# Combining two experts' rows: both choices stacked in the partitions, one matmul per half tile, and scaling two tiles behind

## The chip, the cores and the metric

The kernel runs on one core of a Trainium2 chip. The metric is the device time of one launch in microseconds. Three runs of the kernel before took 2286.6, 2289.5 and 2290.79 us; the median is 2289.5 us. The profile is of one further execution, which took 2287.02 us and whose span in the profile is 2285.2 us.

## The reference, cut to what matters

The model is one layer of a decoder: a mixing part (window attention and a gated delta rule), then a mixture of experts, then a final norm. The change touches only the last step, in which each token's two expert outputs are weighed, summed, added to the residual `h` and normed:

```python
y_buf = lax.map(expert_block, ...)                      # h @ w_down for blocks of 128 rows
y = jnp.zeros((N, D), jnp.float32).at[tok_buf].add(     # two rows for each token
    y_buf.reshape(P, D).astype(jnp.float32) * gate_buf[:, None])
hp = hp + y
y_prompt = rmsnorm(hp, norm_final)                      # x * rsqrt(mean(x*x) + EPS) * gain
```

There are 2048 prompt tokens and 64 sample tokens of width 1024, in float32: 16 tiles of 128 tokens and one of 64, 17 in all.

## The kernel before, in words

The kernel has three stages: a projection, the mixing part, and `moe` (from line 2656). `moe` sorts tokens by expert, runs 66 blocks of 128 rows through the experts (a gate and up product at L3208, a down product at L3217), and writes each result row with an indirect DMA (L2911) to its place in a DRAM tensor `S["y"]`. That tensor holds every token's first choice in one range of rows and every token's second choice in another.

When the last of these writes has landed, ACT signals `experts_stored` (L3004), and the combine begins. This is the stage that the change touches. For each tile `t` of 17:

- SP issues `fetch(t)` (L2832): one DMA brings the rows of 128 tokens, both choices, from `S["y"]` into `pair[t % 8]`, token in the partition, choice as the outer index of the free dimension. It is 1024 KB, in rows of 4 KB, and half of that for the last tile of 64 tokens. Eight buffers stand ready, so eight fetches are issued at once. `fetch(t + 8)` waits until tile `t` has been read (`weighted`).
- ACT makes two diagonal matrices of the 128 tokens' weights, one for each choice (L3011).
- PE (`weigh`, L3243) multiplies: for each half of the 1024 columns, the first choice's rows by the first diagonal and then, accumulating, the second choice's rows by the second. A float32 product shows as two LDWEIGHTS and two MATMUL records, called passes here, so a full tile is 8 passes and the kernel 136. There are four pairs of PSUM banks, so tile `t` waits for `summed` of tile `t - 4`.
- DVE (`add`, L3163) adds `h` and writes `out[t % 8]`. From tile 8 on it waits until the store that used this buffer 8 tiles ago has landed (`stored`).
- ACT squares and sums the row (L3025), POOL makes the root (L2960, L2962).
- DVE scales by the root and the gain (`scale`, L3169). It does this `BEHIND = 4` tiles after the add: after `add(t)` comes `scale(t - 4)`, and after the last add come four more scales.
- SP stores the tile (L2842). SP's program is one list: `fetch(t + 8)`, then `store(t - 4)`, then the same for the next `t`. All fetches and stores go through SP's one queue.

Of the kernel before, what the change touches and what calls it, by code (L numbers as in the profile page):

```python
# [12 lines left out]
ALU = mybir.AluOpType  # L13
ACT = mybir.ActivationFunctionType
AX = mybir.AxisListType.X

P = 128
D = 1024
# [8 lines left out]
HD = 64  # L27
# [2628 lines left out]
def moe(nc, A, S, O, K):  # L2656
# [8 lines left out]
    with Phase(nc, "p5_") as ctx:  # L2665
# [34 lines left out]
        midt = [cut(y_arena, (4 + b) * DE, (FC, P)) for b in two]  # L2700

        CB, OB = 8, 8
        BEHIND = 4
        kept = range(BEHIND + 1)
        pair = [cut(w_arena, 2 * c * D, (2, D)) for c in range(CB)]
        ya = [[pair[c][:, k, :] for c in range(CB)] for k in range(2)]
        out = [cut(w_arena, (2 * CB + c) * D, (D,)) for c in range(OB)]

        n3 = LAST[1] - LAST[0]
# [30 lines left out]
        spare = sb("spare", [P, 3])  # L2740
        home = [sb(f"home{b}", [P, 1], I32) for b in two]
        gain = cut(y_arena, 0, (D,))
        diag = [[cut(y_arena, D + (2 * b + k) * P, (P,)) for k in range(2)] for b in two]
        half = sb("half", [P, 2 * H])
        ss, ms, rs = ([sb(f"{n}{c}", [P, 1]) for c in kept] for n in ("ss", "ms", "rs"))
        ps = ctx.psum([P, 8, 512])
# [26 lines left out]
        def _(sp):  # L2773
# [27 lines left out]
                load_weights(j, j, j % R)  # L2801
            sp.wait_ge(K["ids_out"], 16 * 2 * TILES)
            sp.wait_ge(on["owner_ready"], 1)
            h_flat = h_all[:].rearrange("p t d -> p (t d)")
            with sp.Fori(3 * R, NE - R, R) as i:
                for b in ring:
# [21 lines left out]
            def fetch(t):  # L2828
                r, c = n_rows(t), t % CB
                if t >= CB:  # L2830
                    sp.wait_ge(on["weighted"], t - CB + 1)
                sp.dma_start(pair[c][0:r], S["y"][0:2 * HOMES].rearrange("(k t p) d -> t p k d", k=2, p=P)[t][0:r]  # L2832
                             ).then_inc(gathered[c], 16)

            for t in two:
                fetch(t)
# [131 lines left out]
        @block.scalar  # L2968
        def _(act):
            act.wait_ge(on["shifted"], 1)  # L2970
            nc.scalar.activation(last.ex, last.ex, ACT.Exp).then_inc(on["exps"], 1)

            def gate(j, b):
                act.wait_ge(gu_done.sem, gu_done.all(j))
                act.wait_ge(mid_ready.sem, mid_ready.back(j, 2))
                nc.scalar.activation(th[b], ps[:, 2 + b, 0:DE], ACT.Tanh, scale=0.5).then_inc(th_ready.sem, 1)  # L2976

            def evacuate_y(j, b, sent):
                act.wait_ge(down_done.sem, down_done.all(j))
                act.wait_ge(y_out[b], sent)  # L2980
                nc.scalar.copy(y[b][:, 512:], ps[:, 1 if b else 6, :]).then_inc(y_act.sem, 1)  # L2981

            def blocks(i, first=0):
                for n in range(first, R):
                    gate(i + n, n % 2)
                    evacuate_y(i + n - 1, (n + 1) % 2, 8 * i + 16 * ((n + 1) // 2))

            gate(0, 0)
            act.wait_ge(on["owner_ready"], 1)
            with nc.allow_non_contiguous_dma(reason="the owners of the blocks to one row"):  # L2990
                act.dma_start(owner[0:1, 0:2 * SPILL].rearrange("o (p c) -> o p c", c=2), owner_c[0:SPILL]).then_inc(on["owner_in"], 16)
            act.dma_start(owner[0:1, 2 * SPILL:], total_c[0:1, :]).then_inc(on["owner_in"], 16)
            act.sem_inc(on["owner_in"], 16)
            blocks(0, 1)
            with act.Fori(R, NE - R, R) as i:
                blocks(i)
            total = n_blocks(act)
            with act.Fori(NE - R, total, R) as i:
                blocks(i)
            evacuate_y(total - 1, 1, total * 8)  # L3000
            for b in two:
                act.wait_ge(y_out[b], total * 8 + 16)
            apart(act, on["owner_in"], 48)
            act.sem_inc(on["experts_stored"], 1)  # L3004

            def weights(t):
                n = t if t < SAMPLES else SAMPLES if t == NT else t + 1
                if t >= 2:
                    act.wait_ge(on["weighted"], t - 1)
                for k in range(2):  # L3010
                    nc.scalar.activation(diag[t % 2][k], ident[:], ACT.Copy, scale=w[:, n, k:k + 1]).then_inc(on["diag_ready"], 1)  # L3011

            for t in two:
                weights(t)
            for t in range(T):
                c = t % len(kept)
                if t + 2 < T:
                    weights(t + 2)
                act.wait_ge(on["summed"], t + 1)
                if t >= len(kept):  # L3020
                    act.wait_ge(on["rs_ready"], t - len(kept) + 1)
                if t:
                    act.wait_ge(on["squared"], t)
                r = n_rows(t)
                nc.scalar.activation(y[0][0:r], out[t % OB][0:r], ACT.Square, accum_out=ss[c][0:r]).then_inc(on["squared"], 1)  # L3025

        @block.vector
        def _(dve):
# [124 lines left out]
            with dve.Fori(NE - R, total, R) as i:  # L3153
                blocks(i)
            evacuate_y(total - 1, 1, total * 8)
            dve.wait_ge(on["h_in"], 16 * (NE // R - 2))

            def add(t):
# [22 lines left out]
        @block.tensor  # L3181
        def _(pe):
            mm, tr = nc.tensor.matmul, nc.tensor.transpose
            pe.wait_ge(on["both_ready"], 1)
            pe.wait_ge(on["zero_ready"], 1)
            pe.wait_ge(on["sums_in"], 32)
            earlier(mm, ps[:, 3, :], last, upto, ones).then_inc(on["counted"], 1)

            pe.wait_ge(on["lists_in"], 16)
            mm(ps[:, 7, 0:NE], lists, ident[0:NE, 0:NE], start=True, stop=False)  # L3190
            pe.wait_ge(on["at_ready"], 1)
            for n in range(n3):
                for k in range(2):
                    t = mm(ps[:, 7, 0:NE], at_lane[:, n, k, :], at_block[:, n, k, :], start=False, stop=(n == n3 - 1 and k == 1))  # L3194
            t.then_inc(on["listed"], 1)
            pe.wait_ge(on["sel_ready"], 1)
            pe.wait_ge(on["token_ready"], 1)
            for g in range(4):
                t = mm(ps[:, 4, g * NE:(g + 1) * NE], sel[:, g].rearrange("p q b -> p (q b)"), token, start=True, stop=True)  # L3199
            t.then_inc(on["spread"], 1)  # L3200

            def gate_up(j, b, bw, arrived):
                pe.wait_ge(xt_ready.sem, xt_ready.all(j))
                pe.wait_ge(mid_ready.sem, mid_ready.back(j, 2))
                pe.wait_ge(gate_in[bw], arrived)
                pe.wait_ge(up_in[bw], arrived)
                for c in range(KC):
                    t = mm(ps[:, 2 + b, :], xt[b][:, c, :], w_gu[bw][:, :, c, :], start=(c == 0), stop=(c == KC - 1))  # L3208
                t.then_inc(gu_done.sem, 1)

            def down(j, b, bw, arrived):
                pe.wait_ge(midt_ready.sem, midt_ready.all(j))
                pe.wait_ge(down_in[bw], arrived)
                for n in two:
                    pe.wait_ge(y_act.sem if n else y_vec.sem, y_vec.back(j, 2))
                    for c in range(FC):
                        t = mm(ps[:, n if b else 5 + n, :], midt[b][:, c, :], w_dn[bw][:, c, n * 512:(n + 1) * 512],  # L3217
                               start=(c == 0), stop=(c == FC - 1))
                    t.then_inc(down_done.sem, 1)

            def blocks(i, first=0):
                for n in range(first, R):
                    gate_up(i + n, n % 2, n, 4 * i + 16)
                    down(i + n - 1, (n + 1) % 2, (n - 1) % R, 4 * i + (16 if n else 0))

            gate_up(0, 0, 0, 16)
            blocks(0, 1)
            with pe.Fori(R, NE - R, R) as i:
                blocks(i)
            total = n_blocks(pe)  # L3230
            with pe.Fori(NE - R, total, R) as i:
                blocks(i)
            down(total - 1, 1, R - 1, total * 4)

            def weigh(t):
                c, r, at = t % CB, n_rows(t), 2 * (t % 4)
                pe.wait_ge(on["diag_ready"], 2 * t + 2)
                pe.wait_ge(gathered[c], 16 * (t // CB + 1))
                if t >= 4:
                    pe.wait_ge(on["summed"], t - 3)  # L3240
                for n in two:
                    for k in range(2):
                        ins = mm(ps[0:r, at + n, :], diag[t % 2][k][0:r, 0:r], ya[k][c][0:r, n * 512:(n + 1) * 512],  # L3243
                                 start=(k == 0), stop=(k == 1))
                ins.then_inc(on["weighted"], 1)

            for t in range(T):
                weigh(t)
# [78 lines left out]
```

## Time and profile before

| what | us |
|---|---|
| median of three runs | 2289.5 |
| the profiled execution's own time | 2287.02 |
| its span | 2285.2 |
| busy in the span: PE, DVE, ACT, POOL | 2168.0, 1296.6, 548.6, 612.7 |
| the combine: first fetch issued | 2203.56 |
| the combine: first matmul, last matmul ends | 2208.49, 2270.08 |
| the last scaling ends | 2277.3 |

How to read it: times are from the span's start. The busy time of PE is that of matmuls. The DMA share is the mean busy share of the core's 16 DMA engines in a stretch, and GB/s what they moved. The granted clock of TensorE is given as a part of its full 2.4 GHz.

### The profile page before, as it was taken

To read this page: it belongs to the slowest core of one execution; us is meant where nothing else is said; L and a number is where in the kernel's file an instruction comes from. 1 tells how busy PE (TensorE), PEld (TensorE's weight loads), DVE (VectorE), ACT (ScalarE), POOL (GpSimd) and SP (SyncE) were. 2 spreads that over 40 slices of the span, in tenths; PEclk is the share of its full clock that TensorE was granted. 3 is DMA by queue.
4 is the path that set the end of the run, shared out by engine and by line. 5 is a ranking of instruction groups with operands and counts; after the bars stand their busy time and mean duration, and the time that the engine had idled before them with its cause. 6 is when DMAs were issued, how large, how long until landed. Compare 5 with 4: busy or idle time off the path is not lost. (4 is left out here: it accounts for less than half of the span.)

```text
span 2285.2 us, 47478 instructions
## 1 busy us (share of the span) xinstructions
PE 2168.0 (95%) x18764; PEld 1176.5 (51%) x18764; DVE 1296.6 (57%) x2674; ACT 548.6 (24%) x1421; POOL 612.7 (27%) x804
## 2 busy tenths in 40 slices
PE   7999999999988899999999999839999999999977
PEld 4444544544545666666766666524444444444433
DVE  4524425313524666556676867357767676776736
ACT  3302202202213344334434444200000001010013
POOL 1100200100200100300131221246555555555452
PEclk9999999999998899999999999959999999999988
DMA  9051040230075532233223221159999999999957
GB/s 323 20 148 38 24 148 28 51 115 13 5 206 154 134 101 70 64 86 102 75 65 117 74 65 55 58 228 357 351 373 363 370 365 379 367 383 369 346 206 307
DMA packets 171954, 405.90 MB, mean 178 GB/s; under 512 B 51188, under 2 KB 92772, under 8 KB 147162
## 3 DMA queue, kind: packets, MB, share of 16 engines
q1 hardware_dynamic: 141847, 349.34, 43.5%
q0 software_dynamic: 23648, 35.19, 4.2%
q10 hardware_dynamic: 6274, 18.72, 2.1%
q8 instruction: 139, 2.28, 0.4%
q14 instruction: 46, 0.37, 0.0%
HBM read 344.98 MB, written 94.80 MB: 192 GB/s over the span
## 5 line engine op out<-in xcount | busy, mean ns | idle before, releaser
L3208 PE MATMUL p_ps<-p_w_arena,k_room 128*128 128x512 f32 x1024 | 451.7, 594 | 10.8 <-DVE k_room L3110 10.8
L3208 PEld LDWEIGHTS p_ps<-p_w_arena,k_room 128*128 128x128 f32 x1024 | 195.3, 191 | 256.5 <-issue 245.5
L2864 POOL DMA_INDIRECT k_room<-s_hn,p_slot x272 | 276.4, 1016 | 123.7 <-issue 72.0
L2474 PE MATMUL p_ps<-k_room,p_mixt 128*128 128x512 f32 x544 | 263.5, 614 | 0.0
L3132 DVE STREAM_TRANSPOSE p_y_arena<-p_y_arena 32x64 f32<-32x64 f32 x1024 | 241.0, 235 | 13.2
L902 PE MATMUL p_ps<-k_room,p_w 128*128 128x512 f32 x544 | 240.6, 598 | 0.0
L902 PE MATMUL p_ps<-p_xt,p_w 128*128 128x512 f32 x544 | 238.1, 593 | 0.5 <-DVE p_xt L721 0.5
L3217 PE MATMUL p_ps<-p_w_arena,p_y_arena 128*128 128x512 f32 x512 | 231.9, 596 | 3.5 <-DVE p_y_arena L3132 3.5
L902 PEld LDWEIGHTS p_ps<-k_room,p_w 128*128 128x128 f32 x544 | 102.0, 191 | 124.1 <-issue 122.1
L902 PEld LDWEIGHTS p_ps<-p_xt,p_w 128*128 128x128 f32 x544 | 101.5, 190 | 122.6 <-issue 120.3
L3217 PEld LDWEIGHTS p_ps<-p_w_arena,p_y_arena 128*128 128x128 f32 x512 | 97.8, 191 | 127.3 <-issue 127.3
L3110 DVE STREAM_TRANSPOSE k_room<-k_room 128x1024 f32<-128x1024 f32 x66 | 134.0, 2030 | 13.3 <-DMA k_room<-s_hn,p_slot 11.4
L2474 PEld LDWEIGHTS p_ps<-k_room,p_mixt 128*128 128x128 f32 x544 | 94.6, 190 | 83.7 <-issue 79.1
L731 DVE TENSOR_SCALAR p_y<-p_ext,p_w_conv 128x512 f32<-128x512 f32 x48 | 23.4, 486 | 195.0 <-ACT p_ext L579 195.0
L2976 ACT ACTIVATE p_y_arena<-p_ps 128x256 f32<-128x256 f32 x64 | 24.6, 384 | 440.9 <-PE p_ps L3208 380.7
L2911 POOL DMA_INDIRECT s_y<-k_room,p_home x66 | 68.6, 1039 | 196.1 <-DMA s_y<-k_room,p_home 80.2
L579 ACT COPY p_ext<-p_ps 128x512 f32<-128x512 f32 x48 | 28.1, 586 | 358.0 <-PE p_ps L902 357.9
L3116 DVE SCALAR_TENSOR_TENSOR p_y_arena<-p_y_arena,p_ps 128x256 f32<-128x256 f32 x64 | 26.9, 420 | 148.6 <-ACT p_y_arena L2976 144.9
L735 DVE SCALAR_TENSOR_TENSOR p_y<-p_ext,p_w_conv,p_y 128x512 f32<-128x512 f32 x144 | 108.3, 752 | 5.1
L1517 POOL TENSOR_SCALAR p_ms<-p_ss 128x8 f32<-128x8 f32 x17 | 3.4, 199 | 338.4 <-DVE p_ss L1969 338.4
L522 POOL TENSOR_SCALAR p_ms<-p_ss 128x1 f32<-128x1 f32 (+1 forms) x17 | 6.9, 407 | 296.7 <-ACT p_x L562 196.1
L2981 ACT COPY k_room<-p_ps 128x512 f32<-128x512 f32 x64 | 37.5, 586 | 199.6 <-PE p_ps L3217 187.4
(442 smaller groups left out, 3002.2 us busy)
## 6 DMA issues: line engine op xcount, KB each, us to landing
p_w_arena<-in_w_exp_gate SPq DMA_DIRECT2D x64, 1024.0 KB
p_w_arena<-in_w_exp_up SPq DMA_DIRECT2D x64, 1024.0 KB
p_w_arena<-in_w_exp_down SPq DMA_DIRECT2D x64, 1024.0 KB
p_w_arena<-s_y SPq DMA_DIRECT2D x16, 1024.0 KB, 14.7
p_x<-in_x_prompt SPq DMA_DIRECT2D x30, 512.0 KB, 4.8
s_kv<-p_us SPq DMA_DIRECT2D x32, 256.0 KB
s_kq<-p_y SPq DMA_DIRECT2D x32, 256.0 KB, 3.0
p_kq<-s_kq SPq DMA_DIRECT2D x16, 512.0 KB, 5.8
```

The costliest lines, as they stand in the source:

```text
L579: nc.scalar.copy(ext[q % 3][:, CW - 1:], ps[:, job % 4, :]).then_inc(freed_act.sem, 1)
L735: ins = stt(y[:, c, :], src[:, k:k + SN], w_conv[:, c, k:k + 1], y[:, c, :], ALU.mult, ALU.add)
L902: ins = mm(ps[:, job % 4, :], columns(at, at + P)[:, c], xt[s % 2][:, c, :], start=(c == 0), stop=(c == KC - 1))
L2474: ins = mm(ps[:, 7 - n, :], mixt[t % 2][:, c, :], w_out[:, c, n * 512:(n + 1) * 512], start=(c == 0), stop=(c == KC - 1))
L2864: pool.indirect_dma_start(out=x[b][:, 256 * g:256 * g + 256], out_offset=None, in_=S["hn"].rearrange("t (q k) -> (t q) k", q=4), in_offset ...
L2911: pool.indirect_dma_start(out=S["y"], out_offset=bass.IndirectOffsetOnAxis(ap=home[b][:, 0:1], axis=0), in_=y[b], in_offset=None, bounds_c ...
L2981: nc.scalar.copy(y[b][:, 512:], ps[:, 1 if b else 6, :]).then_inc(y_act.sem, 1)
L3110: nc.vector.transpose(xt[b].rearrange("p c (g r) -> p g c r", g=4), x[bx].rearrange("p (g a c) -> p g c a", g=4, c=KC)).then_inc(xt_ready. ...
L3116: nc.vector.scalar_tensor_tensor(mid[b], th[b], 1.0, ps[:, 2 + b, 0:DE], ALU.add, ALU.mult).then_inc(mid_own.sem, 1)
L3132: t = nc.vector.transpose(midt[b][32 * q:32 * q + 32, :, 32 * g:32 * g + 32], mid[b][32 * g:32 * g + 32].rearrange("p (q a c) -> p q c a", ...
L3208: t = mm(ps[:, 2 + b, :], xt[b][:, c, :], w_gu[bw][:, :, c, :], start=(c == 0), stop=(c == KC - 1))
L3217: t = mm(ps[:, n if b else 5 + n, :], midt[b][:, c, :], w_dn[bw][:, c, n * 512:(n + 1) * 512], start=(c == 0), stop=(c == FC - 1))
```

## The change

A tile is cut into two groups of 64 tokens. `fetch(t)` becomes two DMAs, one for each choice: choice 0 of all the tile's tokens goes to partitions 0 to 63 and choice 1 to partitions 64 to 127, with the group of 64 as the outer index of the free dimension. `weigh` then needs one product for each group and half of the columns, with a stationary operand of 128 rows and 64 columns that holds both choices' weights. Its result goes to 64 partitions of PSUM, the first group's to the lower half and the second group's to the upper. For this ACT makes, in place of two diagonals of 128 columns, two operands of 64 columns from `lanes` (two 64 by 64 identities, one above the other). The weights have to stand in the other half of the partitions too: SP moves them across with two small DMAs (`w_turned`), and DVE puts them together in `w_pair` with four small copies behind `experts_stored`. `BEHIND` goes from 4 to 2.

```diff
-        BEHIND = 4
+        BEHIND = 2
         kept = range(BEHIND + 1)
         pair = [cut(w_arena, 2 * c * D, (2, D)) for c in range(CB)]
-        ya = [[pair[c][:, k, :] for c in range(CB)] for k in range(2)]
...
-        diag = [[cut(y_arena, D + (2 * b + k) * P, (P,)) for k in range(2)] for b in two]
+        diag = [cut(y_arena, D + 2 * HD * b, (2, HD)) for b in two]
+        lanes = cut(y_arena, D + 4 * HD, (HD,))
+        w_pair = cut(y_arena, D + 5 * HD, (T, 2))
+        w_other = cut(K["base"][:], 0, (T, 2))
...
             sp.wait_ge(on["owner_ready"], 1)
+            for a in two:
+                sp.dma_start(w_other[a * HD:(a + 1) * HD].rearrange("p t k -> p (t k)"),
+                             w[(1 - a) * HD:(2 - a) * HD].rearrange("p t k -> p (t k)")).then_inc(on["w_turned"], 16)
...
-                sp.dma_start(pair[c][0:r], S["y"][0:2 * HOMES].rearrange("(k t p) d -> t p k d", k=2, p=P)[t][0:r]
-                             ).then_inc(gathered[c], 16)
+                halves = r // HD
+                for k in two:
+                    sp.dma_start(pair[c][k * HD:(k + 1) * HD, 0:halves],
+                                 S["y"][0:2 * HOMES].rearrange("(k t a p) d -> k t p a d", k=2, a=2, p=HD)[k, t, :, 0:halves]
+                                 ).then_inc(gathered[c], 16)
...
-                for k in range(2):
-                    nc.scalar.activation(diag[t % 2][k], ident[:], ACT.Copy, scale=w[:, n, k:k + 1]).then_inc(on["diag_ready"], 1)
-
+                for a in two:
+                    nc.scalar.activation(diag[t % 2][:, a], lanes, ACT.Copy, scale=w_pair[:, n, a:a + 1]).then_inc(on["diag_ready"], 1)
+
+            act.wait_ge(on["lanes_ready"], 1)
+            act.wait_ge(on["w_paired"], 4)
...
+            dve.wait_ge(on["experts_stored"], 1)
+            tt(lanes, ident[:, 0:HD], ident[:, HD:], ALU.add).then_inc(on["lanes_ready"], 1)
+            dve.wait_ge(on["w_turned"], 32)
+            for k in two:
+                here = slice(k * HD, (k + 1) * HD)
+                nc.vector.tensor_copy(w_pair[here, :, k], w[here, :, k]).then_inc(on["w_paired"], 1)
+                nc.vector.tensor_copy(w_pair[here, :, 1 - k], w_other[here, :, k]).then_inc(on["w_paired"], 1)
             dve.wait_ge(on["h_in"], 16 * (NE // R - 2))
...
-                pe.wait_ge(gathered[c], 16 * (t // CB + 1))
+                pe.wait_ge(gathered[c], 32 * (t // CB + 1))
...
                 for n in two:
-                    for k in range(2):
-                        ins = mm(ps[0:r, at + n, :], diag[t % 2][k][0:r, 0:r], ya[k][c][0:r, n * 512:(n + 1) * 512],
-                                 start=(k == 0), stop=(k == 1))
+                    for a in range(r // HD):
+                        ins = mm(ps[a * HD:(a + 1) * HD, at + n, :], diag[t % 2][:, a], pair[c][:, a, n * 512:(n + 1) * 512],
+                                 start=True, stop=True)
```

## Rows read from the trace of the kernel before

**Rows 1.** The chain that ended last: start us, us, what

```profile
2203.56 4.79 DMA p_w_arena<-s_y
...
2208.49 61.59 PE p_ps L3243 x136
...
2270.10 1.22 DVE p_w_arena L3163
2271.32 4.78 DVE p_w_arena L3169 x4
2276.10 1.20 DVEq L2665
```

**Rows 2.** Stretches: length; busy PE, PEld, DVE, ACT, POOL; PEclk, DMA share, GB/s

```profile
2208.50:2250.00 41.50, 41.50 (x90) 18.25 (x91) 19.40 (x16) 19.09 (x42) 15.73 (x39) 0.93 1.03 404
2260.00:2270.00 10.00, 10.00 (x24) 3.54 (x22) 7.83 (x7) 5.39 (x12) 2.97 (x8) 1.00 0.47 191
```

**Rows 3.** DMA issues of the combine: queue, count, KB each, us to landing

```profile
p_w_arena<-s_y SPq DMA_DIRECT2D x16, 1024.0 KB, 14.7
out_y_prompt<-p_w_arena SPq DMA_DIRECT2D x16, 512.0 KB, 3.4
p_y_arena<-in_norm_final SPq DMA_DIRECT2D x1, 512.0 KB, 8.3
p_w_arena<-s_y SPq DMA_DIRECT2D x1, 512.0 KB, 14.4
```

**Rows 4.** SP's issues in time: a store and the last fetch

```profile
2241.51 0.35 SPq L2842 DMA_DIRECT2D out_y_prompt<-p_w_arena  x1
2242.49 0.65 SPq L2832 DMA_DIRECT2D p_w_arena<-s_y  x1
```

**Rows 5.** PE by line, shapes kept apart: busy us, mean ns of one

```profile
L3243 PE MATMUL p_ps<-p_w_arena,p_y_arena 128*128 128x512 f32 x128 | 58.0, 617 | 10.6 <-DMA p_w_arena<-s_y 10.6
...
L2455 PE MATMUL p_ps<-p_pt,p_av 128*64 128x512 f32 x128 | 31.1, 606 | 0.0
...
L960 PE MATMUL p_ps<-p_w,p_xt 128*64 128x512 f32 x64 | 14.2, 595 | 0.0
```

**Rows 6.** Stretches of 1 us around the last fetch's arrival

```profile
2253.00:2254.00 1.00, 1.00 (x4) 0.50 (x3) 0.06 (x1) 0.64 (x3) 0.74 (x2) 1.00 1.09 352
2254.00:2255.00 1.00, 1.00 (x4) 0.45 (x3) 0.00 (x0) 0.00 (x0) 0.00 (x0) 1.00 1.10 242
2255.00:2256.00 1.00, 1.00 (x3) 0.38 (x2) 0.47 (x1) 0.00 (x0) 0.00 (x0) 1.00 0.91 258
2256.00:2257.00 1.00, 1.00 (x4) 0.49 (x3) 1.00 (x2) 0.21 (x1) 0.00 (x0) 1.00 1.01 414
```

**Rows 7.** Stretches of 1 us while the mixing part loads `w_out` in half tiles

```profile
723.00:724.00 1.00, 1.00 (x12) 1.00 (x14) 0.00 (x0) 0.26 (x1) 0.00 (x0) 0.50 1.05 213
724.00:725.00 1.00, 1.00 (x8) 0.84 (x8) 0.83 (x2) 0.00 (x0) 0.00 (x0) 0.50 1.03 205
725.00:726.00 1.00, 1.00 (x8) 0.84 (x6) 1.00 (x3) 0.00 (x0) 0.00 (x0) 0.51 0.98 197
...
728.00:729.00 1.00, 0.58 (x6) 0.17 (x2) 1.00 (x3) 0.00 (x0) 0.00 (x0) 1.00 0.97 240
```

**Rows 8.** The scaling's group on DVE by line: busy us, mean ns

```profile
L3169 DVE SCALAR_TENSOR_TENSOR p_w_arena<-p_w_arena,p_rs,p_y_arena 128x1024 f32<-128x1024 f32 (+1 forms) x17 | 21.4, 1275 | 0.0
```

**Rows 9.** In order of time: an add, its tile's root; the last tile's root

```profile
2228.76 1.23 DVE L3163 TENSOR_TENSOR p_w_arena<-p_ps,p_h_all 128x1024 f32<-128x1024 f32 x1 [2.21 <-PE p_ps L3243]
...
2231.53 0.55 POOL L2962 TENSOR_TENSOR p_rs<-p_ms,p_half 128x1 f32<-128x1 f32 x1
...
2273.91 1.47 POOL L2962 TENSOR_TENSOR p_rs<-p_ms,p_half 64x1 f32<-64x1 f32 x1
```

**Rows 10.** A small operation on DVE; ACT's diagonals of the first two tiles

```profile
1496.10 0.19 DVE L3041 TENSOR_REDUCE p_h_all<-p_h_all 128x4 f32<-128x32 f32 x1 [0.51 <-ACT p_h_all L2971]
...
2203.62 1.28 ACT L3011 ACTIVATE p_y_arena<-k_ident,k_w 128x128 f32<-128x128 f32 x4 [5.00 <-DMA s_y<-k_room,p_home]
```

## The prediction

> **What bounds the kernel now.** I read the chain of waits first, then the stretches of the combine, then the DMA issues. The chain [rows 1] shows the combine as one piece: the last scattered row lands, the first fetch takes 4.79 us, PE runs 61.59 us without a gap (x136 passes), and then DVE does one add and queued scalings until 2277.30 (2276.10 + 1.20). What follows, up to the end of the span, is 7.9 us of last store and closing (2285.2 - 2277.3), which the change leaves alone. So PE sets the pace. But the stretches [rows 2] show a second limit just under it: from 2208.5 to 2250 the DMA share is 1.03, at 404 GB/s. Only behind the fetches does it fall: 0.47 from 2260 to 2270. The combine's bytes [rows 3] are 16 fetches of 1.049 MB, one of 0.524, the gain's 0.524 and 16.5 stores of 0.524: 26.5 MB, or 65.6 us at 404 GB/s, against PE's 61.6. Two nearly equal limits lie on top of each other: whoever halves one finds the other. The last fetch is issued at 2242.49 [rows 4] and lands 14.4 us later [rows 3], at 2256.9, 13.2 us before PE is done with it.
>
> **The matmuls.** Before, 128 passes of 128 columns are 58.0 us, 0.453 each; the busy time of a group counts overlapping records once. The trace has passes of the new form, alternating between the two halves of the columns: 128 of 128*64 in 31.1 us and 64 in 14.2 us [rows 5], so 0.243 and 0.222 each, while one record's mean (606 and 595 ns) is hardly shorter than that of a full one (617). The two halves run side by side. The new combine has 16 x 8 + 4 = 132 passes: 29 to 32 us in place of 61.6. A tile goes from 8 x 0.453 = 3.6 us to 1.8 to 1.95. Alone, that takes 30 us from PE, and none of it can come off the end beyond what the DMA allows.
>
> **The fetches.** A fetch moves the same bytes in the same 4 KB rows, but as two DMAs of 64 partitions each. That form stands in the trace. The last fetch has 64 tokens and so 64 partitions, [64, 2, 1024] like each new half. Around its arrival [rows 6] the rate is 352, 242 and 258 and then back at 414, with the DMA share still at 0.91 to 1.10: engines busy, moving less. The bytes missing against 410 GB/s, between the mean of the combine and the row behind, are 58 + 168 + 152 = 378 KB, which is 0.92 us on top of 1.28: 0.524 MB took 2.20 us, 238 GB/s. The second place is `w_out`, of which four loads of 512 KB go to 64 partitions each, first twice the lower and then twice the upper half: 205, 197 and later 240 GB/s [rows 7], with the DMA share about 1. So a load to half of the partitions runs at 197 to 258 GB/s. I take 240: the last fetch lies, like each new one, between transfers that don't use only its half, while `w_out` has two of the same half in a row. Ends for the range: 205 GB/s (one of the two slow rows, where the other is a little lower still), and 404, if consecutive DMAs to opposite halves overlap fully.
>
> By the page "SBUF — State Buffer" of the Trainium skill (section "Door 1: The DMA port swizzle (why `[64,N]` ≈ `[32,N]`)"), partitions 0 to 63 reach only 8 of the 16 ports; the two slow places of this trace agree. Its section "Can I just issue two DMAs to hit both halves?" says no, with only 6% over a single one: 1.06 x its 196 GB/s is 208 GB/s, an estimate by that page that would put the sum where the first rival below stands. No row here has two opposite halves in alternation.
>
> **Where that leads.** The 16 full fetches (16.78 MB) take 41.5 us at 404 and 69.9 at 240: +28.4. The DMA queue never runs dry, as eight tiles are asked for ahead and PE now waits for each (at 240 GB/s a tile and its store take 4.4 + 1.3 = 5.7 us, PE 1.9, or twice that if the clock falls to 1.2 GHz in the gaps; DVE 1.22 + 1.27; all of it is covered). Since SP's list has `store(t - 2)` in place of `store(t - 4)`, six stores stand ahead of `fetch(16)` and not four: +2 x 1.3 = +2.6. The last fetch itself is two DMAs of 64 partitions, before one: unchanged. It lands at 2256.9 + 28.4 + 2.6 = 2287.9.
>
> Behind it: `add(14)` needs buffer 6 back, so `store(6)`, next in the queue, landed: 2289.2. DVE then does add(14), scale(12), add(15), scale(13), add(16), at 1.22 [rows 1] and 1.27 [rows 8] each: 6.2, until 2295.4. Two scalings follow (2.5) while ACT and POOL make the last root. Before, the root came 4.06 us after the add (ended 2271.32 [rows 1], root 2273.91 + 1.47 [rows 9]), with POOL slow beside DVE's four scalings; with two I take 3.4 (bounds 4.1 and 2.1, an undisturbed one: add ended 2229.99, root 2232.08 [rows 9]). The last scaling ends at 2295.4 + 3.4 + 1.3 = 2300.1, against 2277.3: **+22.8 us**.
>
> **The scaling two behind.** By itself it takes two of the four queued scalings (2.5 us) from the end and gives most back to the wait for the root: 5.97 us from add to end before, 4.7 after, a gain of 1.3; with the bounds 0.6 to 2.2, the lower by 4.1 + 1.27, the upper where the two scalings' 2.5 end last. It is in the sum.
>
> **Small edits.** SP issues two small DMAs at the start of the expert stage, ahead of block 12's weights, and 17 more fetch DMAs, at 0.35 to 0.65 us each [rows 4]; SP has waits of several us between them, the weights are four blocks ahead: 0 to 1 us, I take 0. DVE's five small operations after `experts_stored` (0.19 each [rows 10], about 0.3 with their semaphores, 1.5 in all) and ACT's first four operands (before 1.28 [rows 10]) come before the first matmul, some 3 us of work under the first fetch's 4.79 [rows 1]: 0. If the cover were gone it would cost 3. In the other direction they could gain nothing, since the fetch is longer than before. The second issue of the first fetch, 0.4, I take as within the 28.4.
>
> **The rivals.**
> 1. *The halves hold to the slowest rate.* At 205 GB/s the fetches take 81.9 us, +40.4 in place of +28.4: **+34.8 us**. For it: the rows of `w_out` and the page above. Against: the last fetch, and 240 in the third row of `w_out`.
> 2. *The engines drift apart.* If the 16 DMA engines need not move in step, one that is a few rows ahead is already on the other half, and it and the one behind no longer hinder each other. At 300 GB/s the fetches take 55.9: +14.4, in all **+8.8 us**. For it: the rows of `w_out` rise from 197 to 240 in three us [rows 7]. Against: after 50 us of traffic the last fetch still showed a sharp dip [rows 6].
> 3. *Opposite halves overlap fully (the other side).* Then the fetches take 41.5. The last lands at 2256.9 + 2.6 - 0.9 = 2258.6, the same 12.2 us follow (2300.1 - 2287.9), end 2270.8: **-6.5 us**. It decides from 16.78 MB / (41.5 + 5.6) = 356 GB/s up, where the sum is zero. For it: bytes and row sizes are the same. Against: the share of busy engines stays at 1 while the rate falls [rows 6, 7].
> 4. *It doesn't do what it says*: the columns' halves run one after another and the fetches at full rate. PE keeps its pace of 0.453 a pass, the last tile has 4 passes fewer (-1.8) and the end gains 1.3: **-3 to 0**, nearly the same. The overlap of the trace speaks against it [rows 5]; under slow fetches it would cost nothing.
>
> **How the numbers follow.** Chances: my forecast (220 to 270 GB/s, +17 to +29) 0.50; rival 1 0.18; rival 2 (270 to 350, +1 to +16) 0.18; rival 3 0.09; rival 4 0.05. The profiled execution took 2287.02, so 2309.8 by the sum; the runs' median lies 2.5 above it, and I give the time against the median: 2289.5 + 22.8 = 2312.3. Range 2294 (+4.5: leaves out rivals 3 and 4 and the edge of 2) to 2326 (rival 1 with 1.5 more). A difference under 0.2% (4.6 us) can't be told from none: faster 0.09, same 0.07 (most of rival 4 and the edge of rival 2), slower 0.84.
>
> **What would show it.** After the change: the rate in the combine at 240 to 300 GB/s (fetches and stores mixed) with the DMA share still at 1; PE busy 29 to 32 us in a stretch of 80 to 90, with waits for `s_y` fetches before nearly every tile and a clock at times at half; a tile every 5.7 us; the adds of tiles 8 to 13 ending right behind a fetch, `scale(16)` some 12 us after the last landing. Wrong if the combine's rate stays at 400, or if PE still runs without gaps.

## The result and the profile after

Over four runs of each, one after another on the same chip, the changed kernel took 2319.2 us (2311.31 to 2320.8) and the kernel before 2288.99 (2286.6 to 2290.79): ratio 1.0131, 95% interval 1.0113 to 1.0148, or **30.2 us slower**. The forecast was 2312.3, the range 2294 to 2326. The profiled execution took 2319.02 with a span of 2317.2, 32.0 over that of before.

I measure the combine from the issue of its first fetch to the end of its last scaling. Before: 2203.56 to 2277.30, 73.7 us [rows 1]. After: 2206.07 to 2308.54, 102.5 us. So 28.7 of the 32.0 lie in it. Another 2.5 lie ahead of it, 1.7 of them already there at the expert stage's first matmul (1532.78 against 1531.08), in code that the change leaves alone. The other 0.8 arose in the expert stage, where the change adds two small DMAs; one execution differs from another by several us up to this point, so no run here says whether they had a part in it, and I count none of the 2.5 as the change's. The remaining 0.8 lies behind the last scaling.

Stretches of the combine after (length; busy PE, PEld, DVE, ACT, POOL; then PEclk, DMA share and GB/s), for [rows 2]:

```profile
2210.00:2220.00 10.00, 4.90 (x12) 1.45 (x14) 1.23 (x1) 1.66 (x4) 7.22 (x18) 0.50 1.05 233
2220.00:2260.00 40.00, 20.90 (x64) 5.07 (x62) 15.72 (x13) 12.83 (x31) 7.97 (x18) 0.80 1.04 216
2260.00:2290.00 30.00, 17.07 (x46) 4.36 (x48) 10.89 (x10) 6.51 (x16) 2.97 (x8) 0.67 1.03 270
2290.00:2300.00 10.00, 6.74 (x16) 1.45 (x12) 6.13 (x6) 4.41 (x10) 1.50 (x5) 0.67 1.02 366
```

This is the whole result in four rows. The share of busy DMA engines is what it was (1.04 against 1.03), and the bytes per second have halved (216 against 404). The share says that the engines are occupied, not that they move much. From 2260 on stores are mixed in, which use all partitions, and the mean rises (270, then 366). PE went from fully busy to about half, and its granted clock from 0.93 to between 0.50 and 0.80.

The DMA issues of the combine after (queue, count, KB each, us to landing), for [rows 3]:

```profile
p_w_arena<-s_y SPq DMA_DIRECT2D x32, 512.0 KB, 24.4
out_y_prompt<-p_w_arena SPq DMA_DIRECT2D x16, 512.0 KB, 20.3
p_w_arena<-s_y SPq DMA_DIRECT2D x2, 256.0 KB, 20.9
```

Sixteen fetches of 1024 KB have become 32 of 512 KB, and a store now takes 20.3 us to land where it took 3.4: it stands behind up to eight tiles of slow fetches in the same queue. The groups of the new combine (line, engine, operation, count | busy us, mean ns | idle before, and what ended it), for [rows 5] and [rows 8]:

```profile
L3260 PE MATMUL p_ps<-p_w_arena,p_y_arena 128*64 128x512 f32 x132 | 50.6, 875 | 50.2 <-issue 27.7 <-DMA p_w_arena<-s_y 20.1 <-ACT p_y_arena L3019 2.4
L3186 DVE SCALAR_TENSOR_TENSOR p_w_arena<-p_w_arena,p_rs,p_y_arena 128x1024 f32<-128x1024 f32 (+1 forms) x17 | 21.7, 1276 | 1.4 <-POOL p_rs L2970 1.4
L3180 DVE TENSOR_TENSOR p_w_arena<-p_ps,p_h_all 128x1024 f32<-128x1024 f32 (+1 forms) x17 | 20.8, 1223 | 59.3 <-PE p_ps L3260 32.5 <-DMA out_y_prompt<-p_w_arena 26.8
```

PE has 132 passes, as counted, and is idle 50.2 us. DVE's operations last what they lasted (1276 and 1223 ns), but its adds wait 26.8 us for stores. Three tiles on PE, eight records each, at two clocks:

```profile
2213.88 3.68 PE L3260 MATMUL p_ps<-p_w_arena,p_y_arena 128*64 128x512 f32 x8 [13.67 <-DMA p_w_arena<-s_y]
2218.78 3.68 PE L3260 MATMUL p_ps<-p_w_arena,p_y_arena 128*64 128x512 f32 x8 [1.22 <-DMA p_w_arena<-s_y]
2230.98 1.94 PE L3260 MATMUL p_ps<-p_w_arena,p_y_arena 128*64 128x512 f32 x8 [2.09 <-DMA p_w_arena<-s_y]
```

A tile is 1.94 us at full clock (2.4 GHz) and 3.68 at half (1.2 GHz): PE had waited 13.67 us before the first. Late in the combine the adds come 5.5 to 6.2 us apart, each released by a store that gave its buffer back:

```profile
2265.52 1.23 DVE L3180 TENSOR_TENSOR p_w_arena<-p_ps,p_h_all 128x1024 f32<-128x1024 f32 x1 [9.34 <-DMA out_y_prompt<-p_w_arena]
2271.69 1.22 DVE L3180 TENSOR_TENSOR p_w_arena<-p_ps,p_h_all 128x1024 f32<-128x1024 f32 x1 [3.76 <-DMA out_y_prompt<-p_w_arena]
2277.14 1.23 DVE L3180 TENSOR_TENSOR p_w_arena<-p_ps,p_h_all 128x1024 f32<-128x1024 f32 x1 [3.03 <-DMA out_y_prompt<-p_w_arena]
```

The end of the chain that ended last (start us, us, what), for [rows 1]:

```profile
2276.32 21.06 DMA out_y_prompt<-p_w_arena
2297.48 1.18 DVE p_w_arena L3180
2298.66 1.15 issue
2299.81 1.23 DVE p_w_arena L3180
2301.07 1.16 ACT k_room L3035 x2
2302.30 2.31 POOL p_ms L2968
2304.68 0.55 POOL p_rs L2970
2305.32 1.28 POOL p_ms L2968
2306.64 0.59 POOLq L2665
2307.26 1.28 DVE p_w_arena L3186
```

Where PE's 61.59 us stood there is now a transfer: `store(6)`, asked for at 2276.32, lands at 2297.4, right behind the last fetch (2296.3). DVE's add(14) waits for it, and the rest is the short tail of adds, the last root and the last scaling.

### The profile page after: what moved, and what is told of

It is laid out like the page before. It is cut to its first block and busy times, and to the rows that moved or that the text cites. A ratio compares the mean times of both kernels' runs of the same rounds, so it can differ in the third digit from the quotient of the medians.

```text
span 2317.2 us, 47498 instructions
## 1 busy us (share of the span) xinstructions
PE 2157.6 (93%) x18760; PEld 1162.9 (50%) x18760; DVE 1297.8 (56%) x2679; ACT 546.7 (24%) x1421; POOL 613.9 (26%) x804
## 5 line engine op out<-in xcount | busy, mean ns | idle before, releaser
L2474 PEld LDWEIGHTS p_ps<-k_room,p_mixt 128*128 128x128 f32 x544 | 94.6, 190 | 83.7 <-issue 79.1
L3260 PE MATMUL p_ps<-p_w_arena,p_y_arena 128*64 128x512 f32 x132 | 50.6, 875 | 50.2 <-issue 27.7
```

The lines of the kernel that those rows point to most:

```text
L2474: ins = mm(ps[:, 7 - n, :], mixt[t % 2][:, c, :], w_out[:, c, n * 512:(n + 1) * 512], start=(c == 0), stop=(c == KC - 1))
L3260: ins = mm(ps[a * HD:(a + 1) * HD, at + n, :], diag[t % 2][:, a], pair[c][:, a, n * 512:(n + 1) * 512], start=True, stop=True)
```

## The experiments

The theory: the fetch in two DMAs of 64 partitions each halves the rate, and this alone makes the kernel slower; the matmuls are twice as fast but hidden, and the scaling two behind gives a little. The rivals: something else in the new combine holds it (the number of DMAs, the order of the list, PE at half clock), or the loss is in the halves only in this order or this queue. Each ratio below is to the kernel before: the first two experiments, the scaling alone and the same matmul over all partitions share 22 runs of it (median 2287.67), the other four share 15 (2288.67).

**One transfer over all partitions.** The changed kernel, but a tile comes as one DMA of 128 partitions (other rows of the same size; the wait is for 16).

```
-                for k in two:
-                    sp.dma_start(pair[c][k * HD:(k + 1) * HD, 0:halves], ...
+                at = 0 if t == NT else t // 8 * HOMES + t % 8 * 2 * P
+                sp.dma_start(pair[c][:, 0:halves],
+                             S["y"][at:at + 2 * P].rearrange("(a p) d -> p a d", a=2)[:, 0:halves]
...
```

> The changed kernel, but each tile's fetch is again one DMA that lands in all 128 partitions: 256 consecutive rows of S["y"] in place of the two choices of the tile's tokens, so the output is that of other rows. Bytes, rows of 4 KB, matmuls, scalings and stores are those of the change. Theory 1 (a load that lands in half of the partitions runs at 210 to 220 GB/s, and that alone costs the time): the combine runs at 400 GB/s again and the kernel is 4 to 9 us faster than before, some 2281 to 2285 us. Rival A (the matmuls of 64 columns, with a clock that falls, or the added chain on DVE and ACT cost the time): it stays 20 us and more above before. Rival B (the number of DMAs in SP's queue costs it): as theory 1, since there is one DMA a tile again.

Measured: 2282.44 us, ratio 0.998 (0.9966 to 0.9995). The combine went from 2202.41 to 2269.77, 67.4 us: 6.4 less than before, where the prediction's third rival had worked out 6.5 for transfers at full rate. Its stretches:

```profile
2220.00:2260.00 40.00, 26.19 (x98) 6.94 (x96) 28.54 (x25) 17.95 (x45) 10.35 (x25) 0.91 1.03 413
```

413 GB/s at a share of 1.03. The bytes, the matmuls, the rest of the list and the scaling are those of the change: all of the 102.5 - 67.4 = 35.1 us between the two hangs on the form of the fetch. Two things differ in that form, the partitions that a DMA reaches and the number of DMAs (one a tile in place of two), and this run can't tell them apart.

**The halves alone.** The kernel before, with nothing changed but the fetch: its own rows in two DMAs of 64 partitions.

```
-                sp.dma_start(pair[c][0:r], ...
+                for a in two:
...
+                    sp.dma_start(pair[c][a * HD:(a + 1) * HD],
+                                 S["y"][0:2 * HOMES].rearrange("(k t p) d -> t p k d", k=2, p=P)[t][a * HD:(a + 1) * HD]
...
-                pe.wait_ge(gathered[c], 16 * (t // CB + 1))
+                pe.wait_ge(gathered[c], 32 * (t // CB + 1))
```

> The kernel before with one thing changed: each fetch is two DMAs, the first 64 tokens (both choices) and the next 64, each to its half of the partitions. Matmuls, diagonals and BEHIND = 4 stay. Theory 1: 16.78 MB at 213 to 220 GB/s take 76 to 79 us in place of 41.5, so the last fetch lands 35 to 37 us later, and behind it come five adds and nine scalings on DVE: 28 to 37 us slower than before, 2317 to 2326 us. Rival A (matmuls and chain): within 3 us of before. Rival B (number of DMAs): as theory 1.

Measured: 2326.92 us, ratio 1.0167 (1.0142 to 1.0193). Its middle stretch and the end of its chain:

```profile
2220.00:2260.00 40.00, 32.93 (x63) 12.92 (x62) 12.71 (x11) 13.48 (x30) 10.23 (x24) 0.87 1.04 219
```

```profile
2313.82 1.22 DVE p_w_arena L3168
2315.04 4.78 DVE p_w_arena L3174 x4
2319.82 1.20 DVEq L2665
```

2210.86 to 2321.02 is 110.2 us, 36.4 over before, at 219 GB/s. The median is 39.3 over that of before, a little more than the 28 to 37 expected. Put the form into the old kernel and the loss appears, take it out of the new one and it is gone. That it is the half of the partitions, and not the doubled number of DMAs, is shown only by the last two experiments below: they too have two DMAs of 512 KB a tile, each over all 128 partitions, and run at 405 and 411 GB/s. The four scalings in a row at the end are still those of [rows 1].

**The scaling alone.** The kernel before with `BEHIND = 2` in place of 4.

> The kernel before with BEHIND = 2 alone. By the prediction 0.6 to 2.2 us faster: two scalings fewer behind the last add, most of it given back to the wait for the last root. If the two further stores ahead of the last fetch mattered, it would be 0 to 2 us slower; they should be hidden, as the last fetch lands 13 us before PE gets to it.

Measured: 2286.18 us, ratio 0.9994 (0.9984 to 1.0005), within the noise. The profile tells more. The end of the chain:

```profile
2217.90 60.82 PE p_ps L3243 x136
2278.74 1.23 DVE p_w_arena L3163
2279.99 1.06 ACT k_room L3025
2281.23 1.17 POOL p_ms L2960
2282.44 0.59 POOLq L2665
2283.05 1.28 DVE p_w_arena L3169
```

From the last add to the end are 5.6 us (2278.74 to 2284.33) in place of 7.2 [rows 1], and 0.8 more comes from PE: in all 71.4 against 73.7, 2.3 less. The four scalings no longer stand ahead of the last; the chain now runs over ACT and POOL, as forecast.

**The same scaling in the slow combine.** The changed kernel with `BEHIND = 4`.

> The changed kernel with BEHIND = 4. The last fetch lands 2.6 us earlier (two stores fewer ahead of it), but behind it the adds of tiles 12 to 16 and the scalings of 8 to 16 remain: 5 adds and 9 scalings, 17.5 us, and 1.3 for the store that frees the first buffer, 18.8 in place of the change's 11.6 measured: about 4.5 us slower than the change, 2323 us. A rival is that the stores ahead of the fetch and the queue of scalings cancel: within 2 us of the change.

Measured: 2321.16 us, ratio 1.0142 (1.0122 to 1.0161). Its stretch of 40 us:

```profile
2220.00:2260.00 40.00, 25.13 (x64) 6.09 (x64) 12.12 (x10) 11.02 (x26) 5.02 (x14) 0.66 1.04 215
```

The combine took 2202.43 to 2310.40, 108.0 us: 5.5 more than with two behind, at the same 215 GB/s. Some 2323 had been expected, 4.5 slower than the change. Against the median of before the two are hard to tell apart (+32.5 over two runs and +30.2 over four); the profiled combine, one execution of each, says that two behind is worth more here than in the old kernel (5.5 against 2.3), where PE paced it.

**Does the order of halves matter?** The changed kernel, but both DMAs of a tile go to the lower half, four tiles ahead instead of eight, as room allows (the upper half's products are of old data).

```
-        CB, OB = 8, 8
+        CB, OB = 4, 8
...
-                    sp.dma_start(pair[c][k * HD:(k + 1) * HD, 0:halves],
+                    sp.dma_start((late if k else pair)[c][0:HD, 0:halves],
```

> The changed kernel with both DMAs of a tile landing in the lower half of the partitions (choice 1 in a buffer of its own, four tiles ahead in place of eight), so the products of the upper half are of old data. If loads to opposite halves, one behind the other, overlap nothing, the rate is that of the change, 213 to 220 GB/s, and the combine as long within 3 us. If they overlap in part (the prediction's second rival), all loads to one half are slower than the change: 200 GB/s or less, 5 us and more.

Measured: 2322.84 us, ratio 1.0149 (1.0128 to 1.017), and 108.2 us of combine (2206.85 to 2315.01). The stretch ahead of the stores (fetches and the one load of the gain), here and, in the second row, in the changed kernel:

```profile
2210.00:2230.00 20.00, 8.37 (x24) 2.29 (x24) 2.45 (x2) 3.47 (x8) 11.16 (x25) 0.67 1.05 212
2210.00:2230.00 20.00, 10.63 (x24) 2.52 (x24) 3.52 (x3) 4.06 (x10) 10.73 (x24) 0.60 1.05 223
```

212 GB/s against 223, 5%. The last fetch lands 98.8 us after the first was asked for, in the change 90.2: of the 8.6 more, 5.2 are four more stores ahead of it, which leaves 3.4 us, 4% of the fetches' time. So alternating halves in one queue buys 4 to 5%, and the smaller number of tiles ahead may be part of it. Neither expectation was met as written: the combine is 5.7 longer, and not within 3, though most of that is stores, and the rate is not down to 200. The page "SBUF — State Buffer" of the Trainium skill, section "Can I just issue two DMAs to hit both halves?", gives 6% for two DMAs at a time to opposite halves over a single one; the 4 to 5% of this pair of runs is near it.

**Two queues.** The changed kernel, but the second choice's half is asked for by ACT, in its own queue.

```
-                for k in two:
...
+                sp.dma_start(pair[c][0:HD, 0:halves], half_of(0, t, halves)).then_inc(gathered[c], 16)
...
+            def fetch_other(t):
+                halves, c = n_rows(t) // HD, t % CB
+                act.dma_start(pair[c][HD:P, 0:halves], half_of(1, t, halves)).then_inc(gathered[c], 16)
```

> The changed kernel with choice 1's half of each fetch issued from ACT's queue, so that loads to the lower and to the upper half stand ready at the same time in two queues. Theory 1, if what counts is where the engines write at one moment: each engine takes from both queues in turn, and the rate rises over the change's 213 to 220, to 250 or more, the time to 2295 to 2310 us. Rival: by the Trainium skill, page "SBUF — State Buffer", section "Can I just issue two DMAs to hit both halves?", two such DMAs in flight gave 6% over one; by that the rate is 225 to 230 GB/s and the time 4 us under the change, about 2315 us. Without the page: the rows of e2, in which the halves alternate in one queue at 216 to 218 GB/s, give the low end, no change at all.

Measured: 2296.34 us, ratio 1.004 (1.0023 to 1.0056). The stretches:

```profile
2210.00:2220.00 10.00, 5.38 (x12) 1.43 (x14) 1.23 (x1) 2.80 (x8) 7.37 (x18) 0.50 1.05 254
2220.00:2260.00 40.00, 24.26 (x86) 6.55 (x82) 18.30 (x16) 14.27 (x34) 7.89 (x20) 0.84 1.03 325
```

325 GB/s over 40 us, some stores among the fetches, and a combine of 83.7 us (2205.10 to 2288.79), 18.8 less than the change: the rate and the time that were expected. So with a queue for each half the transfers overlap in part. It starts at 254 and rises; no run shows what happens between the queues, and none has both queues load the same half, so that the gain comes from the two halves, and not from a second queue as such, is argued and not shown. The same section of the Trainium skill's page says that issuing from several engines doesn't help either; by it this run would have stayed close to the change, and the measurement decides against it here.

**The same matmul, over all partitions.** The two rows of a token can lie in partitions 2p and 2p + 1 rather than p and 64 + p: the matmul sums over the partitions either way. Each group of 64 tokens then comes as one DMA of 512 KB over 128 partitions. The weights must be spread in the same way, and come back by way of DRAM.

```
-                for k in two:
-                    sp.dma_start(pair[c][k * HD:(k + 1) * HD, 0:halves], ...
+                for a in range(r // HD):
+                    sp.dma_start(pair[c][:, a], S["y"][0:2 * HOMES].rearrange("(k t a p) d -> t a p k d", k=2, a=2, p=HD)[t, a]
...
-            tt(lanes, ident[:, 0:HD], ident[:, HD:], ALU.add)
+            tt(lanes, by_two[:, 0], by_two[:, 1], ALU.add)
...
+                for a in two:
+                    for k in two:
+                        sp.dma_start(S["wt"].rearrange("(p k) (a t) -> a k p t", k=2, a=2)[a, k], w[a * HD:(a + 1) * HD, :, k])
```

> The changed kernel, correct, with the two choices of a token in neighbouring partitions (2p and 2p + 1) in place of p and 64 + p: still two DMAs a tile, one for each group of 64 tokens, but each lands in all 128 partitions, 512 KB each. The weights are brought into that order through DRAM, and lanes adds every second column of the identity. Theory 1: full rate, 3 to 8 us faster than before (2281 to 2286 us). Rival B (twice as many DMAs in the queue, each half as large, cost the time): as slow as the change, 2310 us and more. A third outcome, between the two, would say that it matters which partitions an engine writes while the others write theirs, not only how many a DMA reaches.

Measured: 2293.04 us, ratio 1.0024 (1.0008 to 1.004): slower than before, where 3 to 8 us faster had been expected, though the combine took 68.2 us (2214.52 to 2282.68), 5.6 less. Five stretches of the expert stage, from the issue of the weights' pieces at 1632.16 on, and one of its combine:

```profile
1632.00:1636.00 4.00, 4.00 (x10) 1.71 (x9) 3.42 (x14) 0.59 (x1) 2.60 (x4) 1.00 0.61 55
1636.00:1640.00 4.00, 4.00 (x11) 1.80 (x10) 3.03 (x6) 0.00 (x0) 2.75 (x4) 1.00 1.76 4
1640.00:1644.00 4.00, 4.00 (x11) 1.81 (x10) 2.13 (x6) 0.38 (x1) 2.73 (x4) 1.00 1.16 23
1644.00:1648.00 4.00, 4.00 (x10) 1.71 (x9) 3.08 (x14) 0.59 (x1) 0.00 (x0) 1.00 1.00 56
1648.00:1652.00 4.00, 4.00 (x11) 1.78 (x10) 0.00 (x0) 0.38 (x1) 0.00 (x0) 1.00 0.93 90
2220.00:2260.00 40.00, 29.07 (x104) 8.17 (x104) 23.98 (x20) 19.02 (x46) 16.55 (x41) 0.89 1.03 405
```

405 GB/s with two DMAs of 512 KB a tile: the layout does what it should, and the number of DMAs is not what cost the change its rate. The loss is elsewhere. The four DMAs that spread the weights are 4352 pieces of 4 bytes, 17 KB in all, and for some 20 us the engines move 4 to 90 GB/s at a busy share of 0.61 to 1.76. The experts' weights stand behind them in the queue. The same time in the kernel before:

```profile
1636.00:1640.00 4.00, 4.00 (x11) 1.76 (x10) 1.86 (x1) 0.28 (x1) 2.87 (x3) 1.00 1.01 389
1640.00:1644.00 4.00, 4.00 (x11) 1.85 (x10) 3.31 (x11) 0.69 (x2) 1.38 (x3) 1.00 1.02 417
```

If the 16 engines share them evenly, that is 272 pieces each, and an estimate of about 70 ns a piece for the 20 us. Not all of that is the pieces' own time: from 1632 to 1646 the queues carry 4607 packets under 512 bytes, from 1646 to 1652 only 7 of 83, and the rate is still 80 GB/s. Why it stays low behind them is open. The weights that were loaded ahead cover some of the 20 us, and the rest is a stall of PE of 7.35 us:

```profile
1662.01 8.82 PE L3223 MATMUL p_ps<-p_w_arena,k_room 128*128 128x512 f32 x16 [7.35 <-DMA p_w_arena<-in_w_exp_up]
```

**The weights in whole rows.** As the last, but the weights go out as rows of 136 bytes, come back behind the loops into both of a pair's partitions, and DVE picks the even and the odd ones with masks.

```
+            sp.dma_start(S["wt"], w[:].rearrange("p t k -> p (t k)")).then_inc(on["w_turned"], 16)
...
+            for a in two:
+                sp.dma_start(w_both[:, a], S["wt"][a * HD:(a + 1) * HD].unsqueeze(1).to_broadcast([HD, 2, 2 * T]))
...
+            own(nc.vector.tensor_scalar(w_side, both[:, :, 0], even, None, ALU.mult))
+            nc.vector.scalar_tensor_tensor(w_side, both[:, :, 1], odd, w_side, ALU.mult, ALU.add)
```

> The kernel of e4 (choices of a token in neighbouring partitions, each fetch DMA in all 128) with its weights brought over in 384 pieces of 136 bytes in place of 4352 of 4 bytes: w goes to DRAM as it lies, each row comes back to both partitions of its token behind the expert stage's loads, and DVE picks by an even and an odd mask while it waits for the last scatter. In e4 PE stood 7.35 us at 1662 for an expert's weights while the DMA moved 182 GB/s at a share of 0.93: the small pieces held the weights up. Theory 1 (that stall was all that ate e4's gain): no stall in the expert stage, the combine 68 us from the first fetch's issue to the last scaling's end as in e4 (before: 73.7), 4 to 7 us faster than before, 2281 to 2285 us. Rival (something else in e4 delays the combine's start): within 2 us of before or slower.

Measured: **2283.36 us**, ratio 0.9972 (0.9961 to 0.9983): 5.3 us faster than the kernel before, the one full version that beats both. The combine:

```profile
2220.00:2260.00 40.00, 30.15 (x104) 8.22 (x104) 25.26 (x22) 18.12 (x45) 11.54 (x27) 0.83 1.03 411
```

```profile
L3263 PE MATMUL p_ps<-p_w_arena,p_y_arena 128*64 128x512 f32 x132 | 39.9, 728 | 26.0 <-DMA p_w_arena<-s_y 14.2 <-ACT p_y_arena L3022 8.7 <-issue 3.1
```

68.9 us (2206.95 to 2275.81) at 411 GB/s, and no such stall in the expert stage. That the gain is no larger is the prediction's first point: PE's busy time fell from 61.6 to 39.9 us, but the bytes take 65.6 us at 404 GB/s, and they are now what bounds the combine.

## Why the prediction was right, step by step

- **Two limits on top of each other: right.** With PE's work halved and the transfers at full rate (the first experiment) the combine falls only from 73.7 to 67.4 us, against 65.6 for its bytes.
- **The matmuls: passes right, busy time wrong, hidden.** Forecast 29 to 32 us. A tile at full clock is 1.94 us, where 1.8 to 1.95 was forecast, but the busy time is 50.6 us, since the granted clock fell to 0.50 to 0.80 in the gaps. The prediction named the falling clock and the cover, and left the clock out of the busy time. It costs nothing, as PE is idle for another 50.2.
- **The fetch rate: the mechanism right, the size off, and this is nearly the whole miss.** The term was 240 GB/s, +28.4 us. The stretch of fetches alone shows 216. From the landing: the last fetch lands 90.2 us after the first issue (2296.3 - 2206.07), before 53.3 (2256.9 - 2203.56); of the 36.9 more, 2.6 are the two further stores, and 34.3 are the fetches, 75.8 us in place of 41.5, or 221 GB/s. I had read 238 off one transfer of 0.5 MB between two of full width, at the edge of a stretch, and taken the mean of the second place (197 to 240) as a case worse than mine. Apart from the gain's load, eleven tiles in a row have no full-width neighbours until the stores begin. In time, +34.3 lies half way between the prediction's +28.4 and rival 1's +40.4.
- **The two more stores ahead of the last fetch: right by the list.** `store(6)` lands 1.1 us behind the last fetch (2297.4), with 1.3 forecast.
- **The tail: right.** From `store(6)`'s landing to the last scaling 10.9 us were forecast, 11.1 measured (2297.39 to 2308.54). The last root came 3.9 us after its add (ended 2303.35, root 2307.22) with 3.4 forecast and bounds of 2.1 and 4.1.
- **The period of a tile: right, in part by luck.** 5.7 us forecast, 4.4 for the fetches and 1.3 for the store; the adds from 2265.52 to 2294.41 are 5.8 apart. By the landings in this stretch a store takes about 1.15 and the two fetches about 4.7 (224 GB/s), so one part was too small and the other too large. The release was not quite as told: the prediction says behind a fetch, and the profile shows behind a store, which itself lies behind the fetches.
- **The small edits at 0: right for the combine.** DVE's first small operation starts at 2206.08, and the first matmul, waiting for its fetch, at 2213.88. Whether the two small DMAs cost anything in the expert stage is not shown.
- **The sum.** +22.8 forecast; 5.9 more for the rate (34.3 - 28.4), 0.2 less for `store(6)` and 0.2 more for the tail make 28.7, and the combine shows 28.7. That is the upper edge of the +17 to +29 that the forecast was given, half way to rival 1's +34.8, and the medians' 30.2 lies just outside it: the range held for the time because it also took in rival 1.
- **Rivals.** The rate does not rise in one queue, as rival 2 would have it: 216 GB/s holds for 40 us. With two queues it does rise, to 325. Full overlap was refuted for the halves and confirmed, in its sum, where the form is whole (67.4 against 73.7: -6.4 for -6.5). The page of the Trainium skill that spoke against the change ("SBUF — State Buffer", section "Can I just issue two DMAs to hit both halves?") gives, by the prediction's estimate from its figures, 208 GB/s; the trace shows 216 to 221. Why a load to half of the partitions runs at half the rate no run here shows.

## What to carry to other kernels

Look at bytes per second beside the share of busy DMA engines: here loads to half of the partitions kept the share at 1.04 and moved 216 GB/s in place of 404. Where a matmul sums over the partitions, the order of rows in them is free, so choose the one in which every transfer spans all 128, and size a rate from the longest stretch in which such transfers follow one another, not from a single one between others. Halving the engine's work is worth only the distance to the next limit, and a rearrangement in tiny pieces put under cover can cost more than it serves.

## What the runs showed that I had not expected

- Issuing is no longer cheap on a full queue. SP's issues in the changed kernel (start us, us for the count): four of the first take 2.61 us together, late ones about 2 us each, against 0.35 and 0.65 in [rows 4]. It cost nothing that shows, the DMA share staying at 1.04. With four tiles asked for ahead in place of eight (both DMAs to the lower half) the late issues took 0.34 for a store and about 0.6 for a fetch, at the same share, so it seems to hang on how much stands in the queue.

```profile
2206.07 2.61 SPq L2839 DMA_DIRECT2D p_w_arena<-s_y  x4
2255.61 4.14 SPq L2839 DMA_DIRECT2D p_w_arena<-s_y  x2
2276.32 30.59 SPq L2850 DMA_DIRECT2D out_y_prompt<-p_w_arena  x10
```

- Halves from two queues reach 325 GB/s, halves from one 212 to 223, and 512 KB over all partitions 405 to 411. Why the two queues stop at 325 is open.
- 4352 pieces of 4 bytes hold the DMA engines at 4 to 90 GB/s in place of about 400 for some 20 us, some of it after most of the pieces have gone, and stalled PE for 7.35 us.
- The profiled executions reach the combine at 2202.4 to 2214.5 us, up to 12 us apart, in stages that nearly all of these edits leave alone. Only the latest (2214.52) has a reason that was seen, the stall of 7.35; the rest is not explained. So the combines are compared by their own length, and the kernels by medians.
- Not tried: both choices of a token side by side in memory, so that a fetch has rows of 8 KB.
